# Hybrid decoder step on one core: the delta rule ahead of the fox attention, weights loaded piece by piece, V pages in four column strips

## Chip, cores and metric

One NeuronCore of a Trainium2 chip runs the whole step in one launch. The metric is the device time of that launch in microseconds. All data is float32; the large products run as three float32r products of high and low parts.

## What is computed

One layer of a decoder, for a prompt of 512 tokens and for 8 samples of one token each (520 columns in all, `T`). From `xn = RMSNorm(x)` one projection `w_in` feeds four branches and their gates:

```
  A: short gated conv   o_A = Bg * dwconv3(Cg * h)
  B: gated DeltaNet     4 heads (dk=dv=128), causal conv width 4 on q/k/v, per-head decay, delta-rule state, gated RMSNorm output
  C: Conformer conv     GLU -> causal depthwise conv width 31 -> LayerNorm over channels -> swish
  D: forgetting attn    8 heads (d=64), logit[t,s] = q.k/sqrt(d) + sum_{s<j<=t} log f_j, f = sigmoid(w_f.x + b_f)
  x += W_out( sum_i sigmoid(gate_i(xn)) * (o_i @ W_branch_i) )
  x += CrossAttn(RMSNorm(x), memory K/V)   (4 heads x 128 over 256 memory tokens)
  x += ConvFFN(RMSNorm(x))                 (silu(causal dwconv3(x W_g)) * (x W_u)) W_d
```

The samples attend in D to 2048 past tokens each, kept in pages of 128 tokens (16 pages a sample, 128 K pages and 128 V pages of 256 KB, found through a page table). The delta rule goes over the prompt in 4 chunks of 128 tokens; branch C needs 124 taps (31 for each of 4 channel blocks).

## The kernel before

**Weight pieces.** Everything is transposed: channels on partitions, the 520 columns free. `plan()` lists the weights as units of 256 output columns, each cut into two pieces of 128. A piece of `w_in` has 8 row blocks (`kt` = 8), one of `w_branch` 4. There are 208 pieces. For each piece ScalarE makes the high part `wh` of `raw`, POOL (VectorE for `kv` and `cq`) the low part `wl`, and TensorE runs 3 x `kt` matmuls of 260 columns for each half of the columns, into `pb`. "Slot" below is one such half: piece, h. Two units of `raw` and two pieces of `wh` and `wl` are held; the next piece is split while the present one is multiplied. Then ScalarE or VectorE evacuates the tile (`evac`).

**Side steps.** All other work is a list, `SIDE`, of small steps, in order. `timeline()` writes out one order for all engines: behind each slot one side step, then the evacuation, then background work: so many taps of branch C (VectorE, L1618), so many K pages (POOL multiplies by q, L751, VectorE sums per head, L1625), and V pages ahead of a step. Marks in `SIDE` hold a step back (`AFTER` a piece kind) or demand that all steps up to it are done at once, with no pieces between (`BEFORE` a kind): such steps are called bare here. Each engine walks through the same order and waits on semaphores; TensorE runs a side step only when VectorE and ScalarE are through with the ones before it.

The steps that matter: `fox` 0 to 34, the prompt's forgetting attention, one (head, block of 128 queries) a step, as a pipeline of logits, exp, transposes, product with V; `gdn` -1 to 17 for each of four chunks, the delta rule; `gs` the samples' state update; `l2` norms of q and k; `cln` branch C's LayerNorm; `dc`, `ds` decay and softmax of the paged attention, `df` its end; `gp` the output norm of B; `ex` exports; `ml` memory transposes. Pieces go in the order fq, fk, fv, cv/cg, ac/ah/ab, gx (q, k, v of B), then gates and branches A, C, D, gz and B, then `wo`, `kv`, `cq`, cross-attention, `co`, `fg`/`fu`, `fo`.

Before, `fox` runs under the pieces ac to gx, chunk 0 of `gdn` under A's and C's, chunk 1 under C's, and the end of chunk 1, chunks 2 and 3, `gp` and `df` stand bare before `gateD`. A V page is one product of 8 rows by 512 columns:

```
                v_used.by(mm(s3[0:FH, :], sc[:, i, :], kring[:, i % 4, :], i % PAGES == 0, i % PAGES == PAGES - 1))
```

After 16 pages ScalarE copies the 8x512 result and stores it to memory; after the last sample the diagonal blocks are read back and transposed (`df` 0).

## Time and profile before

| | us |
|---|---|
| median of 3 runs (1877.06 to 1886.03) | 1883.24 |
| the profiled execution, its time | 1885.36 |
| its span, first to last instruction | 1883.5 |
| TensorE busy (86% of the span) | 1612.5 |
| VectorE busy (47%) | 876.8 |
| POOL busy (34%) | 633.5 |
| ScalarE busy (30%) | 560.5 |
| mean granted TensorE clock | 0.911 of full speed |

TensorE's busy time counts matmuls whose ends are modelled, so it is not TensorE at its peak. The share is an average: it hides that TensorE is full in some stretches and waits in others. Positions in the text are microseconds from the start of the span.

### The profile page before, as it was taken

What the parts mean: (1) busy time and instruction counts of PE and PEld (TensorE: products, weight loads), DVE (VectorE), ACT (ScalarE), POOL (GpSimd) and SP (SyncE); (2) the same over time, 40 slices, a digit from 0 to 9 for tenths busy, and PEclk for the clock granted to TensorE, in tenths of its full rate; (3) what the DMA queues carried; (4) which work ended last, traced back from release to release, by engine and by line L of the source; (5) the groups of instructions that cost most, each with busy time, mean ns of one, the idle gap of its engine ahead of it and who ended that gap; (6) DMA issues with size and microseconds to landing.
All of it is one profiled execution on the core that took longest, in us unless ns stands there. A gap on an engine that the chain in (4) does not pass through costs nothing. (4 is left out here: it accounts for less than half of the span.)

```text
span 1883.5 us, 28308 instructions
## 1 busy us (share of the span) xinstructions
PE 1612.5 (86%) x11064; PEld 1417.9 (75%) x11064; DVE 876.8 (47%) x1334; ACT 560.5 (30%) x903; POOL 633.5 (34%) x354
## 2 busy tenths in 40 slices
PE   4999899876686678998896899898677999999996
PEld 3899677766575577664343899897566899999995
DVE  4004777777986765313222122255334566664021
ACT  3334232235101322211115223345213333333222
POOL 1337444333466662110000344330402344443341
PEclk8999899877778898999998999999767899999998
DMA  6225322232245442444443522323212222222231
GB/s 196 78 80 176 95 91 96 79 101 90 89 124 179 129 131 67 133 137 140 128 153 102 177 86 78 123 91 101 101 67 68 68 90 90 90 94 82 88 115 46
DMA packets 154389, 200.02 MB, mean 106 GB/s; under 512 B 10180, under 2 KB 112125, under 8 KB 153848
## 3 DMA queue, kind: packets, MB, share of 16 engines
q1 hardware_dynamic: 137253, 169.46, 28.4%
q10 hardware_dynamic: 16011, 24.02, 3.7%
q0 software_dynamic: 992, 4.72, 0.8%
q8 instruction: 88, 1.44, 0.3%
q14 instruction: 45, 0.37, 0.1%
HBM read 187.92 MB, written 10.94 MB: 106 GB/s over the span
## 5 line engine op out<-in xcount | busy, mean ns | idle before, releaser
L740 POOL TENSOR_TENSOR wl<-raw,wh 128x1024 fp32r<-128x1024 f32 (+2 forms) x196 | 427.1, 2179 | 1096.1 <-ACT wh L1105 1094.6
L779 PE MATMUL pb<-xh,wh 128*128 128x260 f32 x2176 | 644.7, 296 | 37.0 <-DVE xl L1480 22.4
L779 PE MATMUL pb<-xl,wh 128*128 128x260 f32 x2176 | 629.8, 289 | 0.0
L779 PE MATMUL pb<-xh,wl 128*128 128x260 f32 x2176 | 628.1, 289 | 0.0
L779 PEld LDWEIGHTS pb<-xh,wh 128*128 128x128 f32 x2176 | 424.7, 195 | 54.7 <-issue 43.3
L779 PE MATMUL sd<-ar 128*128 128x128 f32 (+7 forms) x1584 | 361.4, 372 | 80.0 <-DVE ar L1480 24.7
L779 PEld LDWEIGHTS pb<-xl,wh 128*128 128x128 f32 x2176 | 425.4, 196 | 0.5
L779 PEld LDWEIGHTS pb<-xh,wl 128*128 128x128 f32 x2176 | 425.0, 195 | 0.0
L1105 ACT ACTIVATE wh<-raw 128x1024 fp32r<-128x1024 f32 (+2 forms) x208 | 201.6, 969 | 557.3 <-PE pb L779 530.5
L779 PEld LDWEIGHTS sd<-ar 128*128 128x128 f32 (+4 forms) x1584 | 209.3, 196 | 199.1 <-issue 135.4
L751 POOL TENSOR_TENSOR ar<-ar 128x512 f32<-128x512 f32 x128 | 178.3, 1393 | 95.3 <-DMA ar<-in_cache_fox_k 65.1
L779 PE MATMUL pb<-oh,wh 128*128 128x260 f32 (+1 forms) x384 | 119.0, 310 | 14.4 <-DVE wl L1601 4.6
L783 PE MATMUL sd<-cst,ar 128*128 128x128 f32 (+6 forms) x360 | 66.2, 307 | 63.0 <-DVE ar L1480 26.9
L1618 DVE SCALAR_TENSOR_TENSOR ar<-xT,cols,ar 128x512 f32<-128x512 f32 x120 | 115.7, 1005 | 1.6
L779 PE MATMUL pb<-ol,wh 128*128 128x260 f32 (+1 forms) x384 | 114.7, 299 | 0.0
L779 PE MATMUL pb<-oh,wl 128*128 128x260 f32 (+1 forms) x384 | 114.6, 298 | 0.0
L1625 DVE TENSOR_REDUCE ar<-ar 128x8 f32<-128x512 f32 x128 | 84.8, 679 | 49.5 <-POOL ar L751 49.0
L779 PE MATMUL pb<-hh,wh 128*128 128x260 f32 x352 | 100.8, 286 | 2.6 <-DVE hl L1480 2.6
L783 PEld LDWEIGHTS sd<-cst,ar 128*128 128x128 f32 (+6 forms) x360 | 45.1, 151 | 73.7 <-issue 52.9
L779 PE MATMUL pb<-hh,wl 128*128 128x260 f32 x352 | 100.2, 285 | 0.0
L779 PE MATMUL pb<-hl,wh 128*128 128x260 f32 x352 | 100.2, 285 | 0.0
L779 PE MATMUL sd<-ar,cst 128*128 128x260 f32 (+8 forms) x132 | 46.3, 496 | 56.8 <-DVE ar L1688 20.0
(163 smaller groups left out, 1691.0 us busy)
## 6 DMA issues: line engine op xcount, KB each, us to landing
raw<-in_w_in SPq DMA_DIRECT2D x40, 1024.0 KB, 5.4
ar<-in_cache_fox_k SPq DMA_DIRECT2D x128, 256.0 KB, 2.8
ar<-in_cache_fox_v SPq DMA_DIRECT2D x128, 256.0 KB, 2.8
raw<-in_w_ffn_in SPq DMA_DIRECT2D x22, 1024.0 KB, 5.1
raw<-in_w_branch SPq DMA_DIRECT2D x16, 512.0 KB, 3.5
raw<-in_w_ffn_out SPq DMA_DIRECT2D x8, 1024.0 KB, 5.4
ar<-in_cache_mem_k ACTq DMA_DIRECT2D x1, 4096.0 KB, 19.9
raw<-in_w_out SPq DMA_DIRECT2D x4, 1024.0 KB, 5.2
```

The source lines that it names most:

```text
L740: pool.tensor_tensor(wl[:, p % 2, 0:kt, :], raw[:, u % 2, 0:kt, half * P:(half + 1) * P], wh[:, p % 2, 0:kt, :].bitcast(F32), SUB).then_in ...
L751: own(pool.tensor_tensor(kring[:, i % 4, :], kring[:, i % 4, :], qb[:, :], MUL), prod_done)
L779: return pe.matmul(o, l, r, start=start, stop=stop, skip_group_check=True)
L783: return pe.transpose(o, i, ident[0:n, 0:n])
L1105: own(act.activation(o, i, f, **kw), st)
L1618: dve_c.by(dve.scalar_tensor_tensor(out=oC[:, c, 0:SEQ], in0=g[:, j - 1:j - 1 + SEQ], scalar=w[:, j - 1:j], in1=oC[:, c, 0:SEQ], op0=MUL, ...
L1625: page_free.by(dve.tensor_reduce(sc[:, i, :], kring[:, i % 4, :].rearrange("p (h d) -> p h d", h=FH), AX, ADD))
```

## The change

1. Order of pieces: fq, cv/cg, gx, ac/ah/ab, gates and branches A and C, then fk, fv, gz, gates and branches B and D. Order of steps: `gdn` 0 to 3, each step behind a slot, under ac to fv; then `gp`, and `fox` under gateB, brB and the first gateD piece. Steps `fst`, `fvt`, `fkt` become `fst`, `kvt`; parts of `sm` and `ds` that need fk and fv become `fc` and `dn`. The samples' q is exported by a step `fqr` of its own right behind fq.
2. Weights are loaded piece by piece into a ring of 5, four ahead, and split two ahead. The low part is written over `raw` (name `rawl`), so `wl` is gone. A piece's rows are 128 floats, those of a unit were 256.
3. V pages come in groups of 4, into 8 page buffers. The four products of a group go to rows 0, 32, 64 and 96 of one bank, so to four column strips of the array. After four groups VectorE keeps each head's own block (`vdiag`), four one-column products sum over rows, and VectorE copies the result. The store, the read back and `df` 0 are gone.
4. K pages and taps: 1 tap a slot under gx (2 before), K pages from piece 6 on, 1 to 2 a slot. The state update `gs` takes two samples a step (9 steps for 13).

```diff
-    for n, kind in enumerate(("fq", "fk", "fv")):
+    def heads(n, kind):
         for h in range(2):
             unit("w_in", 0, KD, C_FQ + n * BD + h * 256, kind, 2 * h)
+
+    heads(0, "fq")
     for h in range(2):
         unit("w_in", 0, KD, C_CV + h * 256, "cv", 2 * h)
         unit("w_in", 0, KD, C_CG + h * 256, "cg", 2 * h)
+    for n in range(6):
+        unit("w_in", 0, KD, C_GQ + n * 256, "gx", 2 * n)
     for h in range(2):
         unit("w_in", 0, KD, C_AC + h * 256, "ac", 2 * h)
         unit("w_in", 0, KD, C_AH + h * 256, "ah", 2 * h)
         unit("w_in", 0, KD, C_AB + h * 256, "ab", 2 * h)
-    for n in range(6):
-        unit("w_in", 0, KD, C_GQ + n * 256, "gx", 2 * n)
-    for n, br in enumerate("ACDB"):
+    for br in "ACBD":
         if br == "B":
+            heads(1, "fk")
+            heads(2, "fv")
...
+RING, AHEAD = 5, 2
...
-TAPS_TICK, K_EARLY, K_LATE = 2, 1, (2, 2)
-V_FILLED, V_BARE = 2, 2
-
-
-SIDE = ([("AFTER", "fq")] + [("sm", n) for n in range(4)]
-        + [("AFTER", "fv")]
-        + [("fst", n) for n in range(4)] + [("KSTART",)]
-        + [("fvt", n) for n in range(5)] + [("fkt", n) for n in range(5)]
-        + [("fox", n) for n in range(FOX + 3)]
+VG = 4
+
+
+SIDE = ([("AFTER", "fq", 0)] + [("sm", n) for n in range(4)]
+        + [("AFTER", "fq")] + [("fqr", n) for n in range(2)] + [("KSTART",)]
         + [x for n in range(4) for x in (("AFTER", "gx", 2 * n + 1), ("l2", n))] + [("l2", 4)]
         + [("AFTER", "gx")]
-        + [("gs", n) for n in range(13)]
+        + [("gs", n) for n in range(9)]
+        + [("gdn", n, c) for c in range(2) for n in range(-1, 18)]
         + [("TAPS",)]
-        + [("cln", n) for n in range(7)] + [("BEFORE", "gateC")]
-        + [("gdn", n, 0) for n in range(-1, 12)]
+        + [("cln", n) for n in range(7)] + [("BEFORE", "brC")]
+        + [("gdn", n, 2) for n in range(-1, 18)]
         + [("REDUCES",)]
-        + [("gdn", n, 0) for n in range(12, 18)]
         + [("dc", n) for n in range(3)] + [("ds", n) for n in range(4)] + [("VSTART",)]
-        + [("gdn", n, c) for c in range(1, 4) for n in range(-1, 18)]
-        + [("gp", n) for n in range(5)]
-        + [("PAGES",), ("df", 0), ("df", 1)] + [("BEFORE", "gateD")]
+        + [("gdn", n, 3) for n in range(-1, 2)] + [("BEFORE", "fk")]
+        + [("gdn", n, 3) for n in range(2, 18)]
+        + [("gp", n) for n in range(5)] + [("BEFORE", "gz")]
+        + [("AFTER", "fv")]
+        + [("fst", n) for n in range(2)] + [("dn", n) for n in range(2)] + [("kvt", n) for n in range(5)]
+        + [("fc", n) for n in range(2)]
+        + [("fox", n) for n in range(FOX + 3)]
+        + [("PAGES",), ("df", 1)] + [("BEFORE", "brD")]
...
+MARK_AT = {first_piece("brC") - 1: "brC", first_piece("fk") + 1: "fk", first_piece("gz") + 1: "gz",
+           first_piece("brB") - 1: "brB", first_piece("brD") - 1: "brD", first_piece("wo"): "wo", first_piece("co"): "co"}
...
+TAPS = [(j, c) for pair in range(2) for j in range(CFW) for c in (2 * pair, 2 * pair + 1)]
+N_TAP = len(TAPS)
 N_PAGE = PAGES * NB
+V_OF = PAGES // VG
+V_EVENTS = [x for b in range(NB) for x in [("v", V_OF * b + n) for n in range(V_OF)] + [("vx", b)]]
...
-                background("v", V_FILLED if filled else V_BARE)
+                background("v", step_n[0] % 3 > 0)
...
-        if bg["tap"] is None and p > last_piece("cg") + 1:
+        if p == first_piece("cg") + 2:
             bg["tap"] = 0
         for h in range(2):
             at_piece[0] = p - 1 + h
             out.append(("piece", p, h))
-            if kind in ("gateC", "gateB", "gateD") and p == first_piece(kind) and h == 0:
+            if mark in ("brC", "brB", "brD") and h == 0:
                 evac(p - 1)
-                out.append(("split", "br" + kind[-1]))
+                out.append(("split", mark))
             step(p)
             if h == 0:
                 evac(p - 1)
@@ -307,8 +317,8 @@
                 out.append(("napply", 2, p - first_piece("kv")))
                 if p == last_piece("kv"):
                     out.append(("napply", 2, KD))
-            background("tap", TAPS_TICK)
-            background("k", K_EARLY if p < first_piece("gateA") else K_LATE[h])
+            background("tap", 1 if kind == "gx" else 2)
+            background("k", 1 if kind == "gx" or h == 0 else 1 + p % 2)
...
-        raw = sb("raw", [P, 2, KD, 256])
-        wh, wl = sb("wh", [P, 2, KD, P], F32R), sb("wl", [P, 2, KD, P], F32R)
+        raw_at = -(-nc.sbuf_base // 32) * 32
+        raw = sb("raw", [P, RING, KD, P])
+        rawl = nc.alloc_sbuf_tensor_at("rawl", [P, RING, KD, P], F32R, offset=raw_at)
+        wh = sb("wh", [P, AHEAD + 1, KD, P], F32R)
...
+            def weights(p):
+
+                u, half = PIECES[p][:2]
                 w, row, kt, c = UNITS[u]
-                if u >= 2:
-                    sp.wait_ge(lo.sem, 2 * u - 2)
-                sp.dma_start(raw[:, u % 2, 0:kt, :], W[w][row:row + kt * P, c:c + 256].rearrange("(k p) n -> p k n", p=P))\
-                    .then_inc(raw_in[u % 2], 16)
-
-            def page(cache, i):
+                c += half * P
+                if p >= RING:
+                    sp.wait_ge(piece_done.sem, p - RING + 1)
+                sp.dma_start(raw[:, p % RING, 0:kt, :], W[w][row:row + kt * P, c:c + P].rearrange("(k p) n -> p k n", p=P))\
+                    .then_inc(raw_in[p % RING], 16)
...
+            def v_group(g):
+                for i in range(VG * g, VG * g + VG):
+                    page("cache_fox_v", i, v_slot(i), v_in[i % 8])
...
-                pool.tensor_tensor(wl[:, p % 2, 0:kt, :], raw[:, u % 2, 0:kt, half * P:(half + 1) * P],
-                                   wh[:, p % 2, 0:kt, :].bitcast(F32), SUB).then_inc(lo.sem, 1)
+                pool.tensor_tensor(rawl[:, p % RING, 0:kt, :], raw[:, p % RING, 0:kt, :],
+                                   wh[:, p % (AHEAD + 1), 0:kt, :].bitcast(F32), SUB).then_inc(lo.sem, 1)
...
+                elif kind == "kvt":
+                    for c in range(4):
+                        tr(s0[:, c * P:(c + 1) * P], fv[:, c, n * P:(n + 1) * P])
+                    for c in range(4):
+                        last = tr(s1[:, c * P:(c + 1) * P], fk[:, c, n * P:(n + 1) * P])
+                elif kind == "fc":
+                    for t in range(QT):
+                        last = tr(s0[0:FH, t * P:(t + 1) * P], fltok[:, t, :])
+                elif kind == "dn":
+                    f = qk32[:, :, :].rearrange("p a b -> p (a b)")
+                    mm(s1[:, 0:32], cs(I_LO), f)
+                    last = mm(s1[:, 32:64], cs(I_HI), f)
...
-                        last = mm(s0[:, :], krow[0:32, :], blk[0:32, :, :].rearrange("p a b -> p (a b)"))
+                    else:
+                        for j in range(2):
+                            last = mm(sd[:, j, :], krow[0:32, :], blk[0:32, GH * j:GH * (j + 1), :].rearrange("p a b -> p (a b)"))
...
-            def page(i):
-
-                if i == 0:
+            def v_group(g):
+
+                if g == 0:
                     pe.wait_ge(dve_s.sem, upto(dve_works, ITEMS.index(("ds", 3)) + 1))
-                elif i % PAGES == 0:
-                    pe.wait_ge(v_rows.sem, i // PAGES)
-                pe.wait_ge(page_in[i % 4], 16 * (N_PAGE // 4 + i // 4 + 1))
-                v_used.by(mm(s3[0:FH, :], sc[:, i, :], kring[:, i % 4, :], i % PAGES == 0, i % PAGES == PAGES - 1))
+                elif g % V_OF == 0:
+                    pe.wait_ge(v_out.sem, g // V_OF)
+                for j in range(VG):
+                    i = VG * g + j
+                    pe.wait_ge(v_in[i % 8], 16 * (i // 8 + 1))
+                    last = mm(s3[32 * j:32 * j + FH, :], sc[:, i, :], v_slot(i), g % V_OF == 0, g % V_OF == V_OF - 1)
+                v_used.by(last)
+
+            def v_heads(b):
+
+                pe.wait_ge(v_rows.sem, b + 1)
+                for c in range(KB):
+                    last = mm(s3[:, c:c + 1], vdiag[:, c * P:(c + 1) * P], ones[:, 0:1])
+                v_sum.by(last)
...
+                act.wait_ge(raw_in[p % RING], 16 * (p // RING + 1))
+                if p > AHEAD:
+                    act.wait_ge(piece_done.sem, p - AHEAD)
+                fn(wh[:, p % (AHEAD + 1), 0:kt, :], raw[:, p % RING, 0:kt, :], ACT.Copy, hi)
...
+                elif e[0] == "v" and e[1] % V_OF == V_OF - 1:
+                    dve.wait_ge(v_used.sem, e[1] + 1)
+                    v_rows.by(dve.tensor_tensor(vdiag.rearrange("p (h d) -> p h d", h=FH), s3.rearrange("p (h d) -> p h d", h=FH),
+                                                spread(own_head, FD, 2), MUL))
+                elif e[0] == "vx":
+                    dve.wait_ge(v_sum.sem, e[1] + 1)
+                    own(dve.tensor_copy(vo[:, :, e[1]], s3[:, 0:KB]), v_out)
```

How the order moves. On VectorE, early, before: the taps (L1618) and sums of K pages (L1625) stand between steps of the fox attention (L1675 row maximum, L1679 copy of a result, L1682 and L1483 the division).

```order
L1618 SCALAR_TENSOR_TENSOR ar<-xT,cols,ar 128x512 x2
L1625 TENSOR_REDUCE ar<-ar 128x8
L1675 TENSOR_REDUCE ar<-sd 128x1
L1679 COPY ar<-sd 64x128
L1682 RECIPROCAL ar<-ar 128x1
L1483 TENSOR_SCALAR ar<-ar 128x256
```

Now the taps (L1648) and K sums (L1655) stand between steps of the delta rule (L1760 and L1761, and L1516 the additions to X and its transpose and the next level's mask).

```order
L1648 SCALAR_TENSOR_TENSOR ar<-xT,cols,ar 128x512 x2
L1655 TENSOR_REDUCE ar<-ar 128x8 x2
L1760 TENSOR_TENSOR ar<-ar,sd 128x512
L1761 TENSOR_TENSOR ar<-ar,cst 128x512
L1516 TENSOR_TENSOR ar<-ar,sd 128x512
```

The taps stay where they were in the stream; three delta operations, two of them on the results of products, took the place of four fox ones.

On TensorE, in the bare stretch before `gateD`, before: delta steps (`sd<-ar 128x128`, 4 or 8 products) alternate with V pages (`sd<-ar 8x512`, one product each) and with nothing else.

```order
L779 MATMUL sd<-ar 8x512 x2
L779 MATMUL sd<-ar 128x128 x4
L779 MATMUL sd<-ar 8x512 x2
L779 MATMUL sd<-ar 128x128 x8
L779 MATMUL sd<-ar 8x512 x2
L779 MATMUL sd<-ar 128x128 x4
```

Now the same kind of delta step, with a group of four V pages ahead of it, stands between the weight pieces (`pb` rows; the last and the first rows of a slot are shown).

```order
L802 MATMUL pb<-xh,wh 128x260
L802 MATMUL pb<-xl,wh 128x260
L802 MATMUL pb<-xh,rawl 128x260
L802 MATMUL sd<-ar 8x512 x4
L802 MATMUL sd<-ar 128x128 x4
L802 MATMUL pb<-xh,wh 128x260
L802 MATMUL pb<-xl,wh 128x260
```

24 piece matmuls (12 in a piece of `w_branch`) came between two steps, and the pages come in fours, in two slots of three.

On TensorE, at the last fox steps, now: full steps (logits, forget terms, mask, transposes, product with V) follow each other without a piece between.

```order
L802 MATMUL sd<-ar 128x384
L802 MATMUL sd<-cnh,mask_r 128x384
L802 MATMUL sd<-cnl,mask_r 128x384
L802 MATMUL sd<-mask_r 128x128
L806 MATMUL sd<-cst,ar 128x128 x2
L802 MATMUL sd<-ar 64x128
L802 MATMUL sd<-ar 128x512
L802 MATMUL sd<-cnh,mask_r 128x512
```

Before, each of these had a slot of 24 piece matmuls ahead of it; the last seven steps have lost it, and the delta steps have gained one.

## Rows read from the trace of the kernel before

**Rows 1.** Windows: busy us (instructions) by engine, granted clock, DMA share, GB/s.
```profile
core 0: us, PE busy (x) PEld busy (x) DVE busy (x) ACT busy (x) POOL busy (x), PEclk, DMA share, GB/s
0.00:748.00 748.00, 600.29 (x3963) 534.57 (x3964) 467.06 (x765) 221.19 (x381) 341.78 (x218) 0.88 0.36 113
...
0.00:83.00 83.00, 58.52 (x391) 53.12 (x392) 23.22 (x34) 26.46 (x39) 20.99 (x19) 0.90 0.47 150
...
180.00:326.00 146.00, 135.13 (x859) 108.61 (x857) 110.84 (x207) 42.35 (x90) 64.72 (x40) 0.96 0.29 94
326.00:482.00 156.00, 118.46 (x729) 101.82 (x726) 119.32 (x190) 60.15 (x95) 59.46 (x35) 0.83 0.27 85
482.00:597.00 115.00, 80.76 (x386) 68.73 (x387) 97.92 (x153) 12.17 (x17) 66.90 (x46) 0.71 0.45 138
597.00:748.00 151.00, 113.67 (x836) 110.02 (x835) 95.48 (x145) 40.16 (x64) 82.43 (x57) 0.90 0.37 117
748.00:833.00 85.00, 85.00 (x521) 59.89 (x521) 24.77 (x45) 17.26 (x30) 15.80 (x8) 0.98 0.41 128
833.00:1027.00 194.00, 162.15 (x704) 75.61 (x702) 44.74 (x90) 43.86 (x72) 0.12 (x1) 0.96 0.44 131
```

**Rows 2.** Waits of TensorE from 83 to 748 us: in total, times, longest.
```profile
PE sd L779 <- DVE ar L1480: 20.7, 11, 4.7
PE sd L779 <- DVE ar L1688: 20.0, 3, 10.6
...
PE pb L779 <- POOL wl L740: 11.8, 3, 4.5
```

**Rows 3.** Windows: a stretch of nothing but weight pieces (`fg`, `fu`).
```profile
1550.00:1600.00 50.00, 50.00 (x418) 50.00 (x417) 29.82 (x36) 18.67 (x28) 20.67 (x9) 1.00 0.26 85
```

**Rows 4.** Timeline of TensorE: two V pages, two passes each.
```profile
850.18 1.88 PE L779 MATMUL sd<-ar 128*8 128x512 f32 x4
```

**Rows 5.** Windows: bare delta chunk; chunk 0 under pieces; six `kv` pieces.
```profile
845.00:917.00 72.00, 62.86 (x297) 31.13 (x296) 20.32 (x42) 10.47 (x23) 0.00 (x0) 1.00 0.47 140
621.00:716.00 95.00, 70.51 (x535) 68.79 (x536) 61.92 (x95) 25.44 (x43) 62.05 (x43) 0.89 0.40 125
1281.00:1304.00 23.00, 18.40 (x144) 17.34 (x144) 15.62 (x19) 12.52 (x18) 0.00 (x0) 1.00 0.41 134
```

**Rows 6.** Groups of VectorE from 180 to 410 us: the fox attention's.
```profile
L1483 DVE TENSOR_SCALAR ar<-ar 128x128 f32<-128x128 f32 (+3 forms) x32 | 17.9, 559 | 1.1
L1675 DVE TENSOR_REDUCE ar<-sd 128x1 f32<-128x128 f32 (+3 forms) x32 | 15.6, 487 | 24.6 <-PE sd L779 23.5 <-PE sd L783 0.9
L1679 DVE COPY ar<-sd 64x128 f32<-64x128 f32 x32 | 9.1, 283 | 0.5
...
L1682 DVE RECIPROCAL ar<-ar 128x1 f32<-128x1 f32 x32 | 5.3, 164 | 17.0 <-ACT ar L1105 17.0
```

**Rows 7.** Taps, K products and a delta operation: groups, and two free taps (timeline).
```profile
L1618 DVE SCALAR_TENSOR_TENSOR ar<-xT,cols,ar 128x512 f32<-128x512 f32 x120 | 115.7, 1005 | 1.6
...
L1729 DVE TENSOR_TENSOR ar<-ar,cst 128x512 f32<-128x512 f32 x20 | 15.2, 758 | 0.0
...
L751 POOL TENSOR_TENSOR ar<-ar 128x512 f32<-128x512 f32 x128 | 178.3, 1393 | 95.3 <-DMA ar<-in_cache_fox_k 65.1
...
405.35 1.42 DVE L1618 SCALAR_TENSOR_TENSOR ar<-xT,cols,ar 128x512 f32<-128x512 f32 x2
```

**Rows 8.** Timeline of TensorE: last piece matmul, fox step, next piece.
```profile
293.01 0.28 PE L779 MATMUL pb<-xh,wl 128*128 128x260 f32 x1
...
295.46 0.39 PE L779 MATMUL pb<-xh,wh 128*128 128x260 f32 x1
```

**Rows 9.** Waits of TensorE from 1027 to 1212 us.
```profile
PE pb L779 <- issue: 6.0, 6, 1.0
```

**Rows 10.** DMA issues: count, KB each, us to landing.
```profile
raw<-in_w_in SPq DMA_DIRECT2D x40, 1024.0 KB, 5.4
...
raw<-in_w_branch SPq DMA_DIRECT2D x16, 512.0 KB, 3.5
```

327 lines of the change are left out of this document (159 added, 168 removed).

## Prediction

> **What bounds the kernel now.** I read the windows first [rows 1]. The reader is to see three parts. Behind 1212 us TensorE does little but weight pieces, and the change hardly touches it. From 748 to 1212 us TensorE is 84% to 100% busy. From 180 to 748 us VectorE is the busier engine relative to what it can do: it works 423.5 of 568 us (75%), TensorE loses time and even clock (down to 0.71 between 482 and 597 us).
>
> Then the waits of TensorE [rows 2]: between 83 and 748 us the long ones are on VectorE results (41 us in the two rows); a third, 11.8 us, is on POOL's low parts. So the first half is a VectorE queue that TensorE follows; the middle is TensorE itself.
>
> Then single instructions. In a full stretch 418 matmuls take 50 us [rows 3], 0.1196 us each, so a weight piece of 8 row blocks (48 matmuls) is 5.74 us (5.77 with its edges) and one of 4 blocks 2.88 us. A V page is one 128x512 product of two passes: four passes take 1.88 us [rows 4], 0.94 a page, 120 us for 128 pages, all TensorE time. In the stretch 833 to 1027 us, which has no weight pieces at all, stand 45 or so delta and output-norm steps with 98 V pages; TensorE is still 84% busy there, so hiding those steps under pieces does not return 194 us, only the waits.
>
> **The change part by part.**
>
> *Delta rule under pieces.* One delta chunk stood alone between 845 and 917 us [rows 5]: 72 us, of which 38 pages x 0.94 = 36 are V. The other 36 are the 19 steps. Under pieces the same steps cost less: 748 to 833 us holds 16 steps, 30 pages (28 us) and 8 pieces (4 x 5.74 + 4 x 2.88 = 34.5), which leaves 22.5 us, 1.4 a step, and 25 to 27 for all 19, since three of the last do little on TensorE; I take 25. A chunk therefore saves 36 - 25 = 11 us; 2.2 chunks 24 us, and the four output-norm steps, which wait some 5 us each there, 15 to 20 more. Together about 42 us.
>
> *V strips.* Four pages now go to four column strips of the array and to rows 0, 32, 64 and 96 of one bank. Nothing in the trace shows two strips at once, so I bound it. If each still waits for the other: 3.76 us a group, 120 in all. If the four run as one: 0.94, 30 in all. A page has two passes on one strip that must follow each other; if issue stays in order, page 2's first pass goes with page 1's second, which makes 5 passes of 0.47 instead of 8: 2.3 us a group, 72 in all. I take that, nearest to how rows 4 space passes on one strip. The eight head sums and their copies add about 1 us each, 8 us.
>
> The Trainium skill (TensorE: Matmul & The Clock Gate, Part 3: Packing small matmuls) says that matmuls at different tile positions run at once, a pack lasting one matmul plus some 4 ns a tile. By that rule a group is 0.96 us and the sum below would be 41 us less; no row here shows it.
>
> *First part, to the start of V loading (piece 65).* All 124 taps, all K pages and now three delta chunks stand here; the fox attention is gone from it, and 8 fk and fv pieces. VectorE's work: before, it had 467 us up to 748 us [rows 1]. Fox takes away 17.9 + 15.6 + 9.1 + 5.3 = 48 [rows 6]. Two more chunks add 2 x 21 [rows 5] = 42, and 8 for what they wait on the port (next paragraph). So 469, of which some 34 lie before 83 us (23 before the change, and the gate and decay step, which comes earlier) and 435 behind. At the 75% occupancy of before these take 580 us, at the 85% of the stretch 482 to 597 us 512 us; I take 80%, 544, because each slot now holds one step and fewer taps under gx (2 a piece for 4), so less bunching: the part ends at 627 (595 to 663). TensorE alone would need 39 at the start + 51 x 5.77 + 14 x 2.88 = 335, + 3 x 25 delta + some 41 for the small steps (8 state steps, sums, norms) = 490, so VectorE binds here, as I assumed. The waits of rows 2 are not removed as such; what is left of them is what 627 has over 490.
>
> VectorE also pays for POOL. A tap takes 0.71 us where it is free (1.42 for two) but 1.005 on average over 120, and K products run on POOL for 178 us [rows 7]. The steps moved here have two SBUF operands too (L1729, 20 of them at 0.758). The Trainium skill (SBUF — State Buffer, on the shared port pair) says that such an operation and a GpSimd one exclude each other for the whole instruction; the trace agrees (1.005 against 0.71), and this rule speaks against the move.
>
> By rows: POOL had 342 us up to 748 us [rows 1], and the same products and nearly the same splits stand here after; VectorE's two-operand work is 120 x 0.71 = 85 us of taps, 3 x 11 delta operations x 0.7 = 23, and an estimated 75 for convolutions and the rest (some 105 at 0.7). Were they never to overlap, 525 us: below 544, so it does not decide, but it leaves little.
>
> *Pieces 65 to 96.* TensorE binds (VectorE is at 29% in the like stretch 748 to 833). 22 full pieces 127, 10 half ones 29, delta chunk 25, V 72 + 8, fox 29 steps x 2.55 = 74 (a step under a piece takes 2.45 us from the last piece matmul to the next piece [rows 8], more where it waits), norm, transposes, the new `dn`, `fc` 13. Sum 348.
>
> *Bare fox steps.* The end of the fox line, 29 to 34 and `df`, now has no piece over it. Under a piece a step had the slot's 2.87 + 2.45 = 5.3 us for its whole round through VectorE and ScalarE and often did not wait, so a bare one costs between 2.45 and 5.3 us. Its parts on VectorE alone, one behind the other, are 0.49 + 0.16 + 0.56 [rows 6], so I take the upper end: three full ones, and lighter ones: 28 us (15 at the lower end). Its cover is gone, this is paid whole.
>
> *Pieces 97 to 111.* 7 x 5.77 + 8 x 2.88 = 63, the exports and the memory transpose 12, merged split 3: 78. Before, the six changes from a half to a full piece cost TensorE 1 us each (issue, 6.0) [rows 9]; with two pieces split ahead they go.
>
> *From `wo` on* 1883.5 - 1212.5 = 671. Only the kv pieces gain: six of them take 23 us for 144 matmuls [rows 5], 3.83 each instead of 2.88; VectorE has 1.23 + 0.76 + 0.70 there, so 3.0 is the floor: 7 x 0.8 = 6. So 665.
>
> *Weight loads.* Pieces are now 512 KB of 512-byte rows. Half-height units (512 KB in 512 packets) land in 3.5 us, whole ones (1024 packets) in 5.4 [rows 10]; a piece has the bytes of the first and the packets of the second, so 3.5 to 5.4, issued four pieces (over 11 us) ahead. I cost it at nothing; the cover is that lead.
>
> **Sum.** 627 + 348 + 28 + 78 + 665 = 1746 us of span, 1748 of time against the profiled 1885.4 (which lies 1.9 above its span). That run stands 2.1 above the median of 1883.2, so 1746 against the median: 137 us, 7.3% less.
>
> **The rivals.**
> - *Strips run as one:* V is 30 instead of 72: 1704. For it: each strip has its own bank rows and weights. Against: two passes on a strip. 0.2.
> - *Strips run one after the other:* 120 instead of 72: 1794. For it: no row shows an overlap. 0.2.
> - *VectorE lags as before:* 75% occupancy or less in the first part, taps and delta steps and POOL on one port: it ends at 663 or later: 1782 to 1800. For it: rows 2 and 7. 0.15.
> - *Slower than before:* each of the 57 delta steps in the first part sends TensorE through VectorE's queue, behind two taps and one or two reductions. Chunk 0 did so before, 621 to 716 us, with VectorE at 65% [rows 5]. The gain is gone when the part ends 137 us later, at 764: VectorE would be 435 of 681 us busy, 64%. At 60% it ends at 808 and the time is 1927. Against: chunk 0 then stood at two K reductions in each slot, and TensorE's own work filled the rest. 0.04.
> - *The change does nothing:* V pages were hidden anyway? No: TensorE was 100% busy from 748 to 833. 0.01.
>
> **Numbers.** The forecast case has 0.4. The range 1680 to 1815 holds it and most of the first three rivals; its ends add up the bounds of two terms (595 for 627 and 1704's strips: 1672; 663 and 120: 1830), each drawn in a little. The forecast's own range is 1715 to 1775. What this measurement can tell from no change is about 0.5%, 9 us. Faster 0.94, same 0.02, slower 0.04.
>
> **What would show it.** In the changed profile: four V pages as 8 passes within 2.3 us (0.94 or 3.76 for the rivals); no stretch of TensorE without pieces before `cq` but one of about 28 us with fox steps; piece 65 reached near 627 us, VectorE about 80% busy until then; from there to `wo` 454 us with TensorE nearly full; kv pieces at 3.0 us. I am wrong if VectorE's occupancy in the first part leaves 75 to 85%, if a V group leaves 0.9 to 3.8 us, or if `raw` landings stop pieces.

## The result, and the profile after

The changed kernel takes 1837.38 us (median of 4 runs, 1835.67 to 1845.83), the kernel before 1881.88 (1877.06 to 1886.03): a ratio of 0.9771, 95% interval 0.975 to 0.9792. It is 44 us, 2.3%, faster, where 137 us, 7.3%, were forecast; the time lies above the range of 1680 to 1815. The profiled execution has a span of 1834.5 us against the 1746 of the sum, 88 more.

The first fence is the windows view of the changed kernel, split as the terms of the prediction's sum are: up to piece 65, the same without the start, one delta chunk (the third, pieces 52 to 61), pieces 65 to 96, the bare fox steps, pieces 97 to 111, and the rest. Columns are those of [rows 1].

```profile
core 0: us, PE busy (x) PEld busy (x) DVE busy (x) ACT busy (x) POOL busy (x), PEclk, DMA share, GB/s
0.00:687.50 687.50, 529.09 (x3764) 505.05 (x3765) 497.81 (x713) 188.77 (x283) 345.32 (x216) 0.87 0.40 115
84.00:687.50 603.50, 473.01 (x3425) 455.29 (x3425) 469.72 (x660) 158.86 (x234) 326.87 (x198) 0.87 0.39 113
572.00:653.70 81.70, 72.77 (x580) 71.70 (x581) 53.85 (x83) 25.10 (x44) 45.01 (x31) 0.94 0.40 117
687.50:1062.80 375.30, 337.77 (x2232) 267.12 (x2232) 99.82 (x218) 114.41 (x217) 65.06 (x32) 0.90 0.45 135
1062.80:1092.70 29.90, 20.82 (x71) 12.48 (x69) 5.43 (x17) 4.82 (x13) 0.00 (x0) 0.57 0.07 18
1092.70:1168.20 75.50, 68.89 (x566) 67.44 (x565) 21.09 (x34) 26.03 (x41) 29.85 (x15) 0.99 0.52 156
1168.20:1834.50 666.30, 588.61 (x4499) 574.46 (x4499) 293.41 (x372) 221.80 (x340) 203.63 (x91) 0.92 0.28 87
```

| term | forecast | measured | off by |
|---|---|---|---|
| to piece 65 | 627 | 687.5 | +60.5 |
| pieces 65 to 96 | 348 | 375.3 | +27.3 |
| bare fox steps | 28 | 29.9 | +1.9 |
| pieces 97 to 111 | 78 | 75.5 | -2.5 |
| from `wo` on | 665 | 666.3 | +1.3 |

The reader is to see that all of the miss is in the first two terms, and that they look different. Up to piece 65 VectorE is 78% busy (469.7 of 603.5 us behind 84 us). From 65 to 96 it is 27% busy, TensorE 90%, and yet the clock is only 0.90: TensorE stops often for something short. The waits of TensorE in the two stretches (us in total, times, longest), the first:

```profile
PE sd L802 <- DVE ar L1516: 33.9, 15, 5.0
PE sd L802 <- DVE ar L1720: 27.7, 3, 10.4
PE sd L802 <- ACT ar L1362: 14.9, 3, 8.3
PE pb L802 <- ACT ar L1145: 11.5, 3, 7.0
PE sd L802 <- ACT ar L1335: 9.6, 1, 9.6
```

and those of pieces 65 to 96 (687 to 1063 us):

```profile
PE sd L802 <- DVE ar L1519: 18.4, 9, 2.9
PE sd L802 <- DVE ar L1516: 7.2, 3, 4.1
PE sd L802 <- DVE ar L1522: 3.7, 2, 2.5
```

L1519 in the second is the fox attention's division by the row sum, which TensorE's transposes need. The forecast had none of these nine waits. The timeline of VectorE at one of them (fox step 7, behind the last V group of the sixth sample) shows why:

```profile
919.21 0.69 DVE L1970 TENSOR_TENSOR ar<-sd,cols 128x512 f32<-128x512 f32 x1 [6.26 <-PE sd L802]
919.82 0.55 DVE L1707 TENSOR_REDUCE ar<-sd 128x1 f32<-128x384 f32 x1
920.40 0.29 DVE L1711 COPY ar<-sd 64x128 f32<-64x128 f32 x1
921.19 0.16 DVE L1714 RECIPROCAL ar<-ar 128x1 f32<-128x1 f32 x1 [0.49 <-ACT ar L1145]
921.39 0.42 DVE L1519 TENSOR_SCALAR ar<-ar 128x384 f32<-128x384 f32 x1
```

L1970 takes the diagonal blocks of a sample's V result, so it waits for the V group, and the V group stands behind the piece on TensorE. It idles 6.26 us, and behind it in VectorE's order waits the row maximum (L1707), whose logits TensorE had finished before the piece. Everything that should lie under the piece comes behind it.

The V group itself is short. Timeline of TensorE, changed kernel, four pages of two passes:

```profile
918.03 1.04 PE L802 MATMUL sd<-ar 128*8 128x512 f32 x8
```

Against 1.88 for two pages in [rows 4]. The taps, two convolution operations (L1536, L1519) and the delta rule's mask (L1761) became dearer than in [rows 7] (groups of VectorE, 84 to 687.5 us):

```profile
L1648 DVE SCALAR_TENSOR_TENSOR ar<-xT,cols,ar 128x512 f32<-128x512 f32 x120 | 134.5, 1152 | 1.2
L1655 DVE TENSOR_REDUCE ar<-ar 128x8 f32<-128x512 f32 x128 | 84.7, 677 | 39.6 <-POOL ar L773 38.9
L1536 DVE SCALAR_TENSOR_TENSOR ar<-ar,cols 128x512 f32<-128x512 f32 x44 | 41.3, 938 | 0.6
L1519 DVE TENSOR_SCALAR ar<-ar,cols 128x520 f32<-128x520 f32 x16 | 16.8, 1050 | 4.4 <-ACT ar L1145 4.3
...
L1761 DVE TENSOR_TENSOR ar<-ar,cst 128x512 f32<-128x512 f32 x15 | 15.2, 1017 | 0.0
```

Weights land in 4.1 us (page, DMA issues), within the 3.5 to 5.4 taken from [rows 10], and six `kv` pieces take what they took in [rows 5]:

```profile
raw<-in_w_in SPq DMA_DIRECT2D x80, 512.0 KB, 4.1
```

```profile
1237.40:1260.40 23.00, 19.69 (x144) 18.79 (x144) 15.63 (x19) 12.51 (x18) 0.00 (x0) 0.93 0.42 121
```

### The profile page after: what moved, and what is told of

The parts are those of the page before. It is cut to its first block and busy times, and to the rows that moved or that the text cites. A ratio compares the mean times of both kernels' runs of the same rounds, so it can differ in the third digit from the quotient of the medians.

```text
span 1834.5 us, 28395 instructions
## 1 busy us (share of the span) xinstructions
PE 1545.2 (84%) x11127; PEld 1426.6 (78%) x11127; DVE 917.6 (50%) x1353; ACT 555.8 (30%) x893; POOL 643.9 (35%) x354
## 5 line engine op out<-in xcount | busy, mean ns | idle before, releaser
L762 POOL TENSOR_TENSOR rawl<-raw,wh 128x1024 fp32r<-128x1024 f32 (+2 forms) x196 | 428.6, 2188 | 1040.4 <-ACT wh L1145 1038.8
L802 PE MATMUL pb<-xh,rawl 128*128 128x260 f32 x2176 | 632.0, 290 | 0.0
L802 PEld LDWEIGHTS pb<-xh,rawl 128*128 128x128 f32 x2176 | 429.9, 198 | 0.0
L802 PE MATMUL sd<-ar 128*128 128x128 f32 (+5 forms) x1584 | 280.9, 372 | 96.2 <-DVE ar L1516 37.2
L1648 DVE SCALAR_TENSOR_TENSOR ar<-xT,cols,ar 128x512 f32<-128x512 f32 x120 | 134.5, 1152 | 1.2
L802 PE MATMUL pb<-oh,rawl 128*128 128x260 f32 (+1 forms) x384 | 116.8, 304 | 0.0
L806 PE MATMUL sd<-cst,ar 128*128 128x128 f32 (+7 forms) x359 | 64.2, 302 | 51.0 <-DVE ar L1516 26.4
L1655 DVE TENSOR_REDUCE ar<-ar 128x8 f32<-128x512 f32 x128 | 84.7, 677 | 39.6 <-POOL ar L773 38.9
L1145 ACT ACTIVATE ar<-ar 128x520 f32<-128x520 f32 (+8 forms) x71 | 41.6, 586 | 195.3 <-DVE ar L1542 166.9
L802 PE MATMUL pb<-hh,rawl 128*128 128x260 f32 x352 | 99.5, 283 | 0.0
L802 PE MATMUL sd<-ar,cst 128*128 128x260 f32 (+7 forms) x132 | 43.9, 473 | 65.1 <-DVE ar L1720 27.7
```

The lines of the kernel that those rows point to most:

```text
L762: pool.tensor_tensor(rawl[:, p % RING, 0:kt, :], raw[:, p % RING, 0:kt, :], wh[:, p % (AHEAD + 1), 0:kt, :].bitcast(F32), SUB).then_inc(lo ...
L802: return pe.matmul(o, l, r, start=start, stop=stop, skip_group_check=True)
L806: return pe.transpose(o, i, ident[0:n, 0:n])
L1145: own(act.activation(o, i, f, **kw), st)
L1648: dve_c.by(dve.scalar_tensor_tensor(out=oC[:, c, 0:SEQ], in0=g[:, j - 1:j - 1 + SEQ], scalar=w[:, j - 1:j], in1=oC[:, c, 0:SEQ], op0=MUL, ...
L1655: page_free.by(dve.tensor_reduce(sc[:, i, :], kring[:, i % 4, :].rearrange("p (h d) -> p h d", h=FH), AX, ADD))
```

## The experiments

All ratios are against the kernel before, measured again beside each group of runs, with 95% intervals. e2, e3, e4, e11 and e14 were executed twice, the others four times. "Start of piece 65" is read from the timeline of each. Stretches of two profiles with the same order of work differ by some microseconds: from `wo` on the changed kernel takes 666.3 us and e1 673.1, though the edit of e1 touches nothing there.

### The V pages

**e1_v_behind: VectorE's V operations behind the step.** The order of TensorE and of all other engines stays.

```diff
+def v_behind_steps(order):
+    out = list(order)
+    for j in range(len(out) - 1):
+        e = out[j]
+        if (e[0] == "vx" or e[0] == "v" and e[1] % V_OF == V_OF - 1) and out[j + 1][0] == "side":
+            out[j], out[j + 1] = out[j + 1], e
+    return out
...
-            for e in TIMELINE:
+            for e in v_behind_steps(TIMELINE):
```

> Only VectorE's order changes: its two operations for a sample's V pages (diagonal blocks after the last group, copy after the head sums) stand behind its part of the next side step instead of ahead of it. Theory A: the excess of the slots with them (fox steps 7.2 to 7.7 us against 3.0 to 3.7) is VectorE's row maximum, exp and division waiting in its queue behind the V operation, so that nothing of them lies under the piece. Then these slots fall to 3.7 to 4.2 us, 32 us in 15 slots, and with the clock that is lost behind them 35 to 45 us: near 1797 us. Theory B: the excess is TensorE's own (more products in those slots, weights that come late): no more than 10 us, 1830 or so.

Measured: 1791.17 us, ratio 0.9527 (0.9503 to 0.9551), 46 us below the changed kernel. VectorE's timeline at the same fox step 7:

```profile
890.00 0.56 DVE L1718 TENSOR_REDUCE ar<-sd 128x1 f32<-128x384 f32 x1 [3.61 <-PE sd L813]
890.59 0.29 DVE L1722 COPY ar<-sd 64x128 f32<-64x128 f32 x1
891.38 0.16 DVE L1725 RECIPROCAL ar<-ar 128x1 f32<-128x1 f32 x1 [0.49 <-ACT ar L1156]
891.58 0.42 DVE L1530 TENSOR_SCALAR ar<-ar 128x384 f32<-128x384 f32 x1
892.66 0.69 DVE L1981 TENSOR_TENSOR ar<-sd,cols 128x512 f32<-128x512 f32 x1 [0.66 <-PE sd L813]
```

The same five operations, the V one last (line numbers are 11 higher). The step's slot falls from 8.0 us behind its piece to 4.1. Windows of pieces 65 to 96 and of the bare steps:

```profile
684.20:1004.00 319.80, 308.44 (x2211) 241.97 (x2209) 97.26 (x214) 113.17 (x214) 65.32 (x32) 0.99 0.53 158
1004.00:1036.60 32.60, 23.51 (x92) 15.22 (x92) 6.95 (x21) 6.09 (x16) 0.00 (x0) 0.60 0.06 16
```

319.8 us against 375.3, with nearly the same TensorE instructions, at a granted clock of 0.99 against 0.90. TensorE's idle time fell by 26 us (37.5 to 11.4) and its busy time by 29. Since the products are the same and only VectorE's order changed, these 29 are the lower clock behind the waits: in the changed kernel the piece matmuls behind the wait at step 7 start 0.22 us apart, in e1 0.12 (the lower and the upper of the clock's two levels, 1.2 and 2.4 GHz). So of some 55 us in this stretch half was waiting and half was the clock. Most of it, 42 us, lies in the fox steps. Windows of pieces 82 to 96, in the changed kernel and in e1:

```profile
866.90:1062.80 195.90, 174.38 (x997) 126.91 (x996) 52.57 (x138) 46.70 (x109) 27.67 (x15) 0.86 0.33 97
850.10:1004.00 153.90, 151.95 (x976) 108.79 (x973) 53.84 (x134) 45.45 (x106) 27.75 (x15) 0.99 0.42 123
```

Another 8 lie in delta chunk 3 (104.8 to 97.0 us). Theory A holds, a little above its 45.

**e2_one_strip: four pages on one strip.**

```diff
-                    last = mm(s3[32 * j:32 * j + FH, :], sc[:, i, :], v_slot(i), g % V_OF == 0, g % V_OF == V_OF - 1)
+                    last = mm(s3[0:FH, :], sc[:, i, :], v_slot(i), i % PAGES == 0, i % PAGES == PAGES - 1)
...
-                    last = mm(s3[:, c:c + 1], vdiag[:, c * P:(c + 1) * P], ones[:, 0:1])
+                    last = mm(s3[:, c:c + 1], vdiag[0:FH, c * P:(c + 1) * P], ones[0:FH, 0:1])
```

(VectorE's operation on the diagonal blocks takes rows 0 to 8 alone, too.)

> All four V pages of a group go to rows 0 to 8 of the bank, so to one column strip; everything else is as in the changed kernel. Theory A: strips run at once (a group's 8 passes take 1.04 us in the changed kernel's trace), on one strip they take 8 x 0.47 = 3.76: 32 x 2.7 = 87 us more on TensorE, 70 to 87 of it seen, 1907 to 1924 us. Theory B: the passes are short because pages are in place and products overlap on one strip as well: no more than 15 us slower.

Measured: 1911.35 us, ratio 1.016 (1.0131 to 1.0189): 74 us above the changed kernel and 1.6% slower than before, so theory A. The group of all 256 V passes on TensorE, first on one strip, then in the changed kernel:

```profile
L802 PE MATMUL sd<-ar 128*8 128x512 f32 x256 | 116.9, 599 | 2.0 <-DMA ar<-in_cache_fox_v 2.0
```

```profile
L802 PE MATMUL sd<-ar 128*8 128x512 f32 x256 | 38.2, 598 | 2.1 <-DMA ar<-in_cache_fox_v 2.0
```

The mean of one pass is the same 0.6 us, the time covered by all is 116.9 against 38.2: passes on different strips lie over each other. A group takes 3.65 or 1.19 us on average, so the strips are worth 79 us, and without them the whole change loses. A group that stands alone, on one strip:

```profile
810.60 3.60 PE L802 MATMUL sd<-ar 128*8 128x512 f32 x8
```

The starts of the single passes show how. On one strip the eight start 0.43 us apart. On four strips (the group at 918.03 us above) four start within 0.02 us of each other, and the other four 0.43 us later.

### The first part

**e3_short_k** and **e4_short_taps: less work for POOL, less for VectorE.**

```diff
-                own(pool.tensor_tensor(kring[:, i % 4, :], kring[:, i % 4, :], qb[:, :], MUL), prod_done)
+                own(pool.tensor_tensor(kring[:, i % 4, 0:8], kring[:, i % 4, 0:8], qb[:, 0:8], MUL), prod_done)
```

```diff
-                dve_c.by(dve.scalar_tensor_tensor(out=oC[:, c, 0:SEQ], in0=g[:, j - 1:j - 1 + SEQ], scalar=w[:, j - 1:j],
-                                                  in1=oC[:, c, 0:SEQ], op0=MUL, op1=ADD))
+                dve_c.by(dve.scalar_tensor_tensor(out=oC[:, c, 0:8], in0=g[:, j - 1:j + 7], scalar=w[:, j - 1:j],
+                                                  in1=oC[:, c, 0:8], op0=MUL, op1=ADD))
```

> POOL multiplies 8 instead of 512 columns of each K page (the scores are then not those of the reference); VectorE's sums stay. Theory A: VectorE's work bounds the first part, and a good deal of it is the wait for POOL at the shared port: a tap falls from 1.15 to 0.75 us on average, VectorE's work up to piece 65 by 50 to 60 us, and piece 65 starts near 630 us instead of 687; time near 1780. Theory B: the first part is bound by round trips between the engines, not by VectorE's work: piece 65 no earlier than 670, time 1820 or more.

> The 120 inner taps of branch C run over 8 instead of 512 columns (o_C is then not that of the reference). Theory A (VectorE's work bounds the first part): 120 x (1.15 - 0.2) = 114 us less work, piece 65 near 600 us (TensorE and round trips take over), time near 1750. Theory B (round trips and POOL's queue bound it): piece 65 no earlier than 660, time 1810 or more.

Measured: e3 1788.66 us, ratio 0.9508 (0.9478 to 0.9537), start of piece 65 at 636.6. e4 1808.29 us, ratio 0.9612 (0.9582 to 0.9643), start at 654.4. Groups of VectorE's taps, with short K products and with short taps:

```profile
L1648 DVE SCALAR_TENSOR_TENSOR ar<-xT,cols,ar 128x512 f32<-128x512 f32 x120 | 110.5, 953 | 1.2
```

```profile
L1648 DVE SCALAR_TENSOR_TENSOR ar<-xT,cols,ar 128x8 f32<-128x8 f32 x120 | 66.7, 587 | 1.2
```

A tap of 8 columns still takes 0.587 us on average. In e14 below, where POOL is nearly idle, the same tap takes 0.224 us. So 0.36 of the 0.95 us that e4 was to take from each tap are not the tap's work, but time lost to POOL. e4 removed 63 us of VectorE's time (469.7 to 406.7) and the part became 33 us shorter; e3 removed 62 and the part became 51 shorter. Of e4 neither theory holds as stated, the measurement (654 us, 1808) being close to B (660, 1810), far from A (600, 1750); of e3 theory A holds.

**e11_short_k_low: POOL nearly idle.** On top of e3 (the third product reads the high part, so that there are as many products, and TensorE no longer needs the low part):

```diff
-                pool.tensor_tensor(rawl[:, p % RING, 0:kt, :], raw[:, p % RING, 0:kt, :],
-                                   wh[:, p % (AHEAD + 1), 0:kt, :].bitcast(F32), SUB).then_inc(lo.sem, 1)
+                n = P if p > 64 else 8
+                pool.tensor_tensor(rawl[:, p % RING, 0:kt, 0:n], raw[:, p % RING, 0:kt, 0:n],
+                                   wh[:, p % (AHEAD + 1), 0:kt, 0:n].bitcast(F32), SUB).then_inc(lo.sem, 1)
...
-                    last = mm(o, rawl[:, p % RING, k, :], xa, False, last_ and k == kt - 1)
+                    last = mm(o, (rawl[:, p % RING, k, :] if p > 64 else wh[:, p % (AHEAD + 1), k, :]), xa, False, last_ and k == kt - 1)
```

> On top of e3 (K products of 8 columns): up to piece 64 POOL also makes only 8 columns of each low part, and TensorE's third product of those pieces reads the high part, so that the number of products is the same (results are not the reference's). POOL is then almost idle in the first part. Theory A (the shared port is a price of its own, and VectorE's work the bound): taps fall from 0.95 to 0.75 us, piece 65 starts near 605 us, 80 before the changed kernel and 30 before e3; time near 1760. Theory B (K products were the only disturbance): within 8 us of e3, 1781 or more.

Measured: 1758.04 us, ratio 0.9329 (0.9311 to 0.9348), start of piece 65 at 605.0. Taps and the delta rule's masks (L1761 before):

```profile
L1649 DVE SCALAR_TENSOR_TENSOR ar<-xT,cols,ar 128x512 f32<-128x512 f32 x120 | 85.8, 748 | 1.2
...
L1762 DVE TENSOR_TENSOR ar<-ar,cst 128x512 f32<-128x512 f32 x15 | 10.3, 684 | 0.0
```

Theory A holds. A tap takes 1152, then 953, then 748 ns as POOL's K products and then its low parts go, and a mask 1017 and 684. VectorE's instructions behind 84 us are the same (661, and 660 in the changed kernel). Not separated is what TensorE gains by not waiting for low parts; in the changed kernel it waits for them 4.3 us in the whole part. The Trainium skill (SBUF — State Buffer, on the shared port pair) calls it a lock held for a whole instruction, not shared bandwidth; the trace agrees, since a tap of 8 columns pays nearly as much for POOL (0.587 against 0.224 below) as one of 512 (1.152 against 0.748).

**e14_short_all: all three.** The taps of e4 on top of e11.

> On top of e11 (POOL's K products and low parts short in the first part): the taps run over 8 columns too (results are not the reference's). Theory A (VectorE's work still binds up to piece 48): 120 x (0.75 - 0.2) = 66 us less work, piece 65 near 555 us, time near 1705. Theory B (what is left is TensorE's round trips, 57 delta steps at 1.9 us, l2, gs1 and gdn 0 behind chains of two engines): piece 65 no earlier than 590 and the floor of 490 in the prediction was 100 us too low.

Measured: 1740.37 us, ratio 0.9242 (0.9212 to 0.9272), start of piece 65 at 592.0, so theory B. Windows of its first part behind 84 us, and of the third delta chunk; and its taps:

```profile
84.00:592.00 508.00, 453.58 (x3438) 438.85 (x3437) 297.21 (x661) 159.81 (x239) 57.39 (x198) 0.92 0.46 134
479.70:560.10 80.40, 73.67 (x589) 72.75 (x590) 46.53 (x83) 25.04 (x43) 10.31 (x31) 0.94 0.42 119
```

```profile
L1649 DVE SCALAR_TENSOR_TENSOR ar<-xT,cols,ar 128x8 f32<-128x8 f32 x120 | 23.0, 224 | 1.2
```

VectorE is 59% busy and POOL 11%, and the part still needs 592 us. TensorE is 89% busy; 54 us are waits, at a granted clock of 0.92. The third delta chunk, which has no taps in either kernel, takes 80.4 us with POOL 10.3 us busy, against 81.7 with POOL 45.0: it hardly depends on K products or the port. What the 297 us of work that VectorE still has add to the 592, no run shows.

**e15_before_short_k: the edit of e3 in the kernel before.**

> The kernel before with POOL's K products over 8 columns (scores not the reference's). In the changed kernel the same edit brings 49 us. Theory A (the move raised the price: delta steps' two-operand work stands beside K products now, and VectorE binds more of the time): the kernel before gains 15 to 30 us. Theory B (the price was there all along): 45 us or more.

Measured: 1825.98 us, ratio 0.9688 (0.966 to 0.9716), 57 us less than before; in the changed kernel the edit gave 49. Theory B: the price of the K products on POOL was there all along, and the move did not raise it. (Short K products also free POOL sooner for the low parts and let VectorE's sums start sooner; e3 and e15 take all of this together.)

**e8_norms_later: the four l2 steps two pieces later**, on top of e1.

```diff
-        + [x for n in range(4) for x in (("AFTER", "gx", 2 * n + 1), ("l2", n))] + [("l2", 4)]
+        + [x for n in range(4) for x in (("AFTER", "gx", 2 * n + 3), ("l2", n))] + [("l2", 4)]
```

> On top of e1: each of the four l2 steps stands one unit of gx (two pieces) later. Theory A (place): the four waits of 12 to 14 us are TensorE at a step whose input VectorE's convolution and ScalarE's square have only just been asked for; two pieces later it is there, each slot falls to about 4 us, 4 x 9 = 36 us in all, part of it taken back by VectorE's queue at the next such place: 1755 to 1770 us. Theory B (work, the ground of the prediction): VectorE is 87% busy between 133 and 270 us and sets the pace whatever stands where: no more than 12 us, 1780 or so.

Measured: 1793.64 us, ratio 0.9521 (0.9506 to 0.9537), no difference from e1, so theory B. TensorE's wait on the norms' own operation between 133 and 311 us was 27.7 us in the changed kernel (L1720); here it is:

```profile
PE sd L813 <- DVE ar L1731: 27.2, 3, 10.1
```

The wait moved with the step. TensorE's l2 step waits for VectorE's l2 operation of the same step, which stands in VectorE's order behind all that is ahead of it; a step later in the list is a later place in VectorE's queue too. VectorE is 87% busy from 133 to 270 us in the changed kernel and 88% here, and while it is that far behind this later place is no better; others were not tried.

### Weights

**e5_ahead1: splitting one piece ahead.**

```diff
-RING, AHEAD = 5, 2
+RING, AHEAD = 5, 1
```

> The changed kernel with weight pieces split one ahead instead of two; the ring of 5 and the loads four ahead stay. Theory A (the prediction's: weights cost nothing, what is gained by two ahead is about 1 us at each change from a half to a full piece): ten such changes and the stretch of half pieces, 1840 to 1855 us. Theory B: in the first part, where ScalarE and POOL are late, the second split ahead is what keeps TensorE fed: 1870 or more.

Measured: 1838.26 us, ratio 0.9748 (0.9728 to 0.9767): the changed kernel's time, a little below theory A's 1840. Start of piece 65 at 685.9. Costing the weight pieces at nothing was right. Between 1060 and 1240 us TensorE's waits put down to issue come back (5.2 us in three, none in the changed kernel), but nothing of them can be measured in the whole. TensorE never waits for a landing of `raw`. Its one wait on a low part, 4.3 us at 135 us, has the same form as the one of the V pages: on POOL the low part stands behind two K products that wait 5.7 and 1.6 us for their pages.

### Better versions

**e7_both: K pages one a slot**, `dc` and `ds` behind delta chunk 3, and a V group or V operation at every step instead of two in three, on top of e1.

```diff
-        + [("REDUCES",)]
-        + [("dc", n) for n in range(3)] + [("ds", n) for n in range(4)] + [("VSTART",)]
         + [("gdn", n, 3) for n in range(-1, 2)] + [("BEFORE", "fk")]
         + [("gdn", n, 3) for n in range(2, 18)]
+        + [("REDUCES",)]
+        + [("dc", n) for n in range(3)] + [("ds", n) for n in range(4)] + [("VSTART",)]
...
-                background("v", step_n[0] % 3 > 0)
+                background("v", 1)
...
-            background("k", 1 if kind == "gx" or h == 0 else 1 + p % 2)
+            background("k", 1)
```

> On top of e1: one K page a slot throughout instead of up to two, the end of the K pages with decay and softmax (dc, ds) behind delta chunk 3, and a V event at every step behind that. Theory A: VectorE and POOL have 17 fewer K pages up to piece 52, 17 x (0.68 + 1.4 us on the port at worst): piece 52 some 15 us earlier, dc and ds (3 to 5 us each with VectorE's queue) cheaper by 5: near 1772. Theory B (places, not work): 5 us or less, 1786 to 1791.

Measured: 1779.61 us, ratio 0.9458 (0.9438 to 0.9479), 12 below e1, between theory A (1772) and theory B (1786 or more). Which of the three changes brings it is not shown.

**e9_three** is e7 with the later norms.

> e1, the later norms and the K pages spread, together. If they add: the sum of both gains below 1791, near 1740. If they are worth the same waits: the better of the two, near 1755.

Measured: 1784.47 us, ratio 0.9485 (0.9463 to 0.9506). Neither forecast (1740, 1755) holds: the later norms bring nothing here either.

**e10_pairs: light steps in pairs**, on top of e9; **e16_no_norms** is the same on top of e7.

```diff
                 pos[0] += 1
+                if s in (("fst", 0), ("dn", 0), ("kvt", 0), ("kvt", 2), ("fc", 0)):
+                    continue
                 return
```

> On top of e9: five pairs of light steps (fst, dn, kvt, fc) share a slot, so that the fox attention begins five slots earlier and two of its steps and df are left bare instead of seven. Bare steps cost 4.3 us each (29.9 us for seven with df, at a granted clock of 0.56), under pieces 3.0 to 3.5, and the clock does not fall: 10 to 20 us less than e9. Against it: the second step of a pair waits bare for the first, 5 x 1.5 us.

> e10 without the later norms, which is e7 with the five pairs of light steps. e8 and e9 said that the later norms bring nothing or cost 2 to 5 us: so 1765, 0 to 5 us below e10's 1769, and 10 to 18 below e7's 1780.

Measured: e10 1769.37 us, ratio 0.9403 (0.9384 to 0.9422); e16 1776.19 us, 0.9434 (0.9411 to 0.9457). e10 is 15 us below e9, as forecast (10 to 20); e16 did not come out at its 1765. The pairs bring 15 us over e9 but only 3 over e7, and the intervals of e10 and e16 meet: differences of some 5 us between these versions can't be told apart, and whether the later norms matter beside the pairs stays open.

**e12_k_late** and **e13_k_later: K pages moved behind piece 48**, on top of e16.

```diff
-            background("k", 1)
+            background("k", h if kind == "gx" else 1 if p < 48 else 1 + h)
```

(e13: `h if 11 < p < 40 else 1 if p < 48 else 1 + max(h, p % 2)`.)

> On top of e10 without the later norms: K pages every second slot under gx, one a slot up to piece 48, one and a half behind it. Up to piece 48 there are 12 K pages fewer. Between e1 and e7 piece 48 came 9 us earlier with 16 pages fewer, 0.6 us each, so piece 48 comes 7 us earlier here; behind it VectorE is busy 58% and POOL 55%, so the pages cost nothing there: near 1760. Rival: behind piece 48 POOL's products and low parts (1.5 x 1.45 + 1.33 us in a half piece's two slots) fill its slots and the 7 us are given back: 1767 or more.

> As e12, with K pages every second slot up to piece 40 as well, one a slot to 48, 1.75 behind it: 28 pages fewer than in e10 up to piece 48, 17 us earlier there. Behind it 72 pages in 46 slots: POOL needs 1.75 x 1.45 = 2.5 us a slot for them and 0.7 to 1.25 for the low part, more than a half piece's slot lasts, so some of it comes back: near 1757 if POOL keeps up, 1765 or more if not.

Measured: e12 1768.17 us, ratio 0.9389 (0.9368 to 0.9411); e13 1770.7 us, 0.9399 (0.9379 to 0.942). Windows of e12, then of e13, up to piece 48 and from there to 65:

```profile
84.00:518.40 434.40, 348.00 (x2534) 333.51 (x2533) 347.64 (x497) 117.38 (x169) 214.67 (x122) 0.88 0.37 105
518.40:672.90 154.50, 124.91 (x964) 122.01 (x962) 100.35 (x160) 46.60 (x78) 102.98 (x72) 0.91 0.48 136
```

```profile
84.00:510.10 426.10, 350.80 (x2542) 337.10 (x2541) 334.28 (x481) 118.28 (x174) 192.39 (x105) 0.87 0.34 96
510.10:679.30 169.20, 129.48 (x962) 126.32 (x961) 106.11 (x167) 46.58 (x78) 110.42 (x79) 0.88 0.48 137
```

Later K pages make the first stretch shorter (434, 426) and the second longer (154.5, 169.2): the rivals hold, e12's (1767 or more) and e13's (1765 or more). The profile of e12 is of its fastest run, 7 us below its median, so part of the difference between the two may be that. e12 is the fastest version, with e10 and e13 inside its interval: 69 us below the changed kernel, 6.1% below the kernel before.

## Why the prediction was wrong, point by point

In the sum, two terms failed. VectorE's work in the first part was 469.7 us where 435 were taken, and the V operations, "about 1 us each", left out what waits behind them on VectorE: 55 us in pieces 65 to 96 (e1), of which the strips gave back 34. The reason given for the first of them, that VectorE binds because TensorE needs only 490 us, failed as well.

**"TensorE alone would need ... 490, so VectorE binds here".** e14 takes most of POOL's work and the taps away, and the part still ends at 592. That is 102 us above 490, nearly all of it in three places (e14, read from the slots of its timeline). The start: piece 4 and all that is behind it begin at 84 us, where the sum had 39 and four pieces, 62 (22 more). The delta chunks: beside their pieces (5.77 and 2.88 us each) the three take 34, 31 and 36 us in e14, for 25 each (26 more). The small steps: l2 31, state update 29, norm of C 15, decay and softmax 18, for 41 together (52 more). In four l2 steps and the first steps of each chunk TensorE goes through two other engines and back. The 25 came from steps whose round trips two V pages covered: TensorE was busy for all 85 us from 748 to 833 at a clock of 0.98 [rows 1], and in the third chunk of the changed kernel it is idle for 8.9 of 81.7 at 0.94. In the changed kernel the three chunks take 52, 45 and 39 us beside their pieces, where a bare one takes 36 [rows 5]: the first row of the forecast gain, 11 us a chunk, was not there. (The 335 in that sum is the pieces alone; with the 39 it is 374, which the 490 holds.)

**"At the 85% ... 512 us; I take 80%, 544"** got the occupancy nearly right (78%) and the work wrong: 469.7 us behind 84 instead of 435. Taps at 1.152 for 1.005 are 18 of the 35, the convolutions and the masks most of the rest, and all of these get cheaper in e11, when POOL is nearly idle. At 80% that is 43 us, the occupancy the other 16: 60 in all. The occupancy is a mean of two stretches, though: 83% up to piece 48 (377 of 453.5 us), 62% from there to 65 (92 of 150), where the taps are gone and the round trips bind. One ratio for both was luck, not method. What the taps and POOL cost is what e14 gave back: 95 of the 603 us.

**V strips.** The forecast's 2.3 us a group was too much: 1.19 on average and 1.04 where it stands alone. The rival "strips run as one" was right in this term, at 0.2; 38.2 us of passes against 72 (2.3 x 32 is 74) makes 34 us that came back. The reason given for 2.3, that issue in order would make the second page wait for the first page's second pass, is refuted by the starts under e2: the four pages' passes come in two waves. By the Trainium skill (TensorE: Matmul & The Clock Gate, Part 3: Packing small matmuls) a pack lasts one matmul and a few nanoseconds for each further tile, which gave an estimate of 0.96 for a group; this case's trace has 1.04, so it nearly agrees.

**"Fox 29 x 2.55 = 74"** was right for the step and left out what was queued ahead of it. With e1 the fox steps take 73 us beside their V work (2.6 each, from the slots of its timeline), in the changed kernel 112. The prediction gave the head sums and copies 1 us each, as TensorE's work, and did not ask what else waits in VectorE's order behind an operation that waits for TensorE. Such an operation stands there twice for each sample: 46 us in the whole (e1).

**Pieces 65 to 96** thus come out as 348 - 34 (strips) + 55 (the V operations with the clock, e1) + 7 (delta chunk 3, which takes 32 us for 25 even in e1) - 1 for the rest = 375.

**Bare fox steps, pieces 97 to 111, `wo` on**: within 2.5 us each. In the last the `kv` term was wrong: 6 us were given for splitting ahead, and six pieces take 23.0 us as before. That the stretch came out at its 665 all the same was luck; by e1's 673.1 it is not known better than by some 7 us.

**The rivals.** "VectorE lags" (663 or later) named the place and not the reason: the occupancy was 78%, not 75% or less. "Slower than before" did not come near, but its mechanism, delta steps that send TensorE through VectorE's queue, is part of the miss. Of the two theories for the first part, work and round trips, neither is enough: the reasons add, 95 us for the one and about 100 above the forecast floor for the other.

**The signs of being wrong** that the prediction named did not appear: VectorE's occupancy (78%) and the V group (1.19 us) stayed within their bounds, and no landing of `raw` stopped a piece. None of them looked at VectorE's work, at the 490 or at VectorE's order.

## What to carry to other kernels

When an operation that waits for TensorE is put into another engine's order, look at what stands behind it there: if that is the first link of the next step's chain, the chain loses its cover (here 55 us in one stretch for 16 operations, half of it by a granted clock of 0.90 for 0.99). Put it behind the chain's links: in e1 no new long wait came of it.

Take a step's price under cover from steps that had the cover which they will have, not from steps that had more. And test a floor ("this engine alone would need ...") by adding the waits of every step that goes through two other engines and back, since here the second bound lay 100 us higher than it was reckoned, which was most of the 137 between the two.
